# The long and the short pass of each weight block: issued in turn instead of grouped

## What is computed

```python
def swiglu(x, w_in, w_out):
    a, b = jnp.split(x @ w_in, 2, axis=-1)
    return (jax.nn.silu(a) * b) @ w_out

for l in range(DEPTH_2):                                   # 2 layers
    x = x + 0.5 * rmsnorm_2(swiglu(rmsnorm_2(x, ffn1_pre_g[l]), w_ffn1_in[l], w_ffn1_out[l]), ffn1_post_g[l])
    h = rmsnorm_2(x, mix_pre_g[l])
    (z, xbc, dt_raw, rq, rk, rv, rg, aq, ak, av, gate) = jnp.split(h @ w_in[l], offsets, axis=-1)
    ...                                                    # three mixers: y_ssd, y_ret, y_att
    ys = jnp.stack([y_ssd.astype(x.dtype), y_ret.astype(x.dtype), y_att.astype(x.dtype)], axis=2)
    branch = jnp.einsum('blmc,mcd->blmd', ys, w_branch[l])
    gates = jax.nn.sigmoid((gate + b_gate[l]).reshape(bsz, L, N_BRANCH, D_MODEL))
    y = jnp.sum(gates * branch, axis=2) @ w_out[l]
    x = x + rmsnorm_2(y, mix_post_g[l])
    x = x + 0.5 * rmsnorm_2(swiglu(rmsnorm_2(x, ffn2_pre_g[l]), w_ffn2_in[l], w_ffn2_out[l]), ffn2_post_g[l])
```

## Time and profile before

| | |
|---|---|
| time, median of 3 runs | 2068.77 us (2067.3 to 2069.11) |
| span of the profiled execution | 2065.9 us |
| PE busy | 1909.0 us, 92% |
| PEld busy | 1529.2 us, 74% |
| DVE busy | 1163.1 us, 56% |
| ACT busy | 897.5 us, 43% |
| DMA, mean | 235 GB/s |
| the chain that ended last, by engine | PE 77%, DMA 18% |

### The profile page before, as it was taken

How to read it: one execution, slowest core, us unless ns; L and a number is a source line. 1 busy time by engine, 2 the same in 40 slices (tenths; PEclk the granted TensorE clock), 3 DMA queues, 4 the chain that set the end, 5 groups by cost and what they waited for, 6 DMA issues and landing times.

```text
span 2065.9 us, 29171 instructions
## 1 busy us (share of the span) xinstructions
PE 1909.0 (92%) x11974; PEld 1529.2 (74%) x11974; DVE 1163.1 (56%) x1632; ACT 897.5 (43%) x1338; POOL 43.8 (2%) x99
## 2 busy tenths in 40 slices
PE   8998666766689999999999999999999999999998
PEld 8983222212168888999988988888888999889887
DVE  5761111100056756568876776476674779766763
ACT  5531000000044544568653654454444677645542
POOL 0010000000010000000000000000000000000000
PEclk9999888888799999999999999999999999999999
DMA  8489999999983655534444555445555434455552
GB/s 329 181 329 388 425 428 426 426 427 426 427 352 128 256 187 184 185 122 144 153 171 176 206 187 199 163 165 215 193 183 183 164 123 154 147 180 207 185 194 90
DMA packets 58001, 486.00 MB, mean 235 GB/s; under 512 B 6464, under 2 KB 6464, under 8 KB 7712
## 3 DMA queue, kind: packets, MB, share of 16 engines
q1 hardware_dynamic: 56736, 476.24, 60.6%
q0 software_dynamic: 1152, 8.16, 1.0%
HBM read 483.33 MB, written 1.05 MB: 234 GB/s over the span
## 4 chain that ended last, share of the span: by engine, by line
PE 77%; DMA 18%; ACT 1%; DVE 1%; issue 1%; SPq 0%; POOL 0%; DVEq 0%; ACTq 0%; POOLq 0%
DMA ring<-in_w_experts 16%; PE bank L1644 16%; PE bank L1659 12%; PE bank L1764 11%; PE bank L2022 8%; PE bank L1657 7%; PE bank L1678 4%; PE bank L1694 3%; PE bank L1676 2%; DMA work<-in_w_experts 2%; PE bank L1655 2%; PE bank L1479 1%; PE bank L1127 1%; ACT work L2508 1%; PE bank L1674 1%; PE bank L2229 1%
## 5 line engine op out<-in xcount | busy, mean ns | idle before, releaser
L1617 DVE TENSOR_TENSOR ring_parts<-ring,work_parts 128x2048 fp32r<-128x2048 f32 x168 | 384.5, 2291 | 184.5 <-ACT work_parts L1610 155.1
L1610 ACT ACTIVATE work_parts<-ring 128x2048 fp32r<-128x2048 f32 x118 | 224.9, 1911 | 105.5 <-PE bank L1764 76.7
L1659 PE MATMUL bank<-work_parts 128*128 128x512 f32 x840 | 213.2, 393 | 0.0
L1644 PE MATMUL bank<-pair_parts,ring_parts 128*128 128x256 f32 x672 | 189.9, 283 | 0.0
L1657 PEld LDWEIGHTS bank<-work_parts,ring_parts 128*128 128x128 f32 x1280 | 174.6, 190 | 12.3
L1657 PE MATMUL bank<-work_parts,ring_parts 128*128 128x256 f32 x1280 | 178.5, 282 | 0.0
L1659 PEld LDWEIGHTS bank<-work_parts 128*128 128x128 f32 x840 | 150.1, 189 | 26.2
L1764 PE MATMUL bank<-work_parts 128*128 128x512 f32 x512 | 161.5, 389 | 0.0
L1617 DVE TENSOR_TENSOR ring_parts<-ring,columns_parts 128x2048 fp32r<-128x2048 f32 x56 | 128.3, 2290 | 53.0 <-ACT columns_parts L1610 25.1
L1405 DVE TENSOR_TENSOR work<-work,bank 128x512 f32<-128x512 f32 x8 | 5.5, 688 | 251.8 <-PE bank L1479 251.8
L1479 PE MATMUL bank<-work 128*32 128x512 f32 x512 | 85.5, 804 | 61.6 <-DMA work<-in_w_experts 61.6
(11 more groups left out here) (451 smaller groups left out, 3713.3 us busy)
## 6 DMA issues: line engine op xcount, KB each, us to landing
ring<-in_w_layers SPq DMA_DIRECT2D x242, 1024.0 KB, 4.9
work<-in_w_experts SPq DMA_DIRECT2D x42, 2048.0 KB, 36.2
ring<-in_w_experts SPq DMA_DIRECT2D x36, 1024.0 KB, 23.2
ring<-in_w_experts SPq DMA_DIRECT2D x14, 2048.0 KB, 37.4
work<-in_w_experts SPq DMA_DIRECT2D x20, 1024.0 KB, 10.1
ring<-in_w_first SPq DMA_DIRECT2D x16, 1024.0 KB, 7.9
tail<-in_w_experts SPq DMA_DIRECT2D x7, 2048.0 KB, 40.5
columns<-in_w_experts SPq DMA_DIRECT2D x8, 1024.0 KB, 42.0
```

Of the source, the lines that this page charges most:

```text
L1610: act.activation(his[j % len(his)], m.ring[U.slot(names[j])], ACT.Copy).then_inc(F["unit_hi"], 1)
L1617: dve.tensor_tensor(m.ring_r[slot], m.ring[slot], his[j % len(his)].bitcast(F32), ALU.subtract).then_inc(F["unit_lo"], 1)
L1644: mm = pe.matmul(out, w, x, start=k + n == 0, stop=k == KT - 1 and n == 2)
L1659: mm = pe.matmul(bank[:], hi[:, k, :], both[:, k, :], start=False, stop=k == KT - 1)
```

## The change

In both functions the loop over the weight blocks issues the long and the short matmul of the same block one after the other. The first long one still starts the sum; the last instruction of a job, which ends the sum and carries the semaphore, is now the short one of `k` = 7. The number of matmuls and of weight loads, their operands, the bank, the claim of the bank and the wait for the parts stay.

```diff
@@ wide_columns
-        pe.matmul(bank[:], hi[:, 0, :], both[:, 0, :], start=True, stop=False)
         for k in range(KT):
-            pe.matmul(bank[:, 0:T], lo[:, k, :], both[:, k, 0:T], start=False, stop=False)
-        for k in range(1, KT):
-            mm = pe.matmul(bank[:], hi[:, k, :], both[:, k, :], start=False, stop=k == KT - 1)
+            pe.matmul(bank[:], hi[:, k, :], both[:, k, :], start=k == 0, stop=False)
+            mm = pe.matmul(bank[:, 0:T], lo[:, k, :], both[:, k, 0:T], start=False, stop=k == KT - 1)
         mm.then_inc(B.full(job), 1)
@@ wide_end
-        pe.matmul(halves, hi[:, 0, :], both[0], start=True, stop=False)
         for k in range(KT):
-            pe.matmul(halves[:, first], lo[:, k, :], both[k][:, first], start=False, stop=False)
-        for k in range(1, KT):
-            mm = pe.matmul(halves, hi[:, k, :], both[k], start=False, stop=k == KT - 1)
+            pe.matmul(halves, hi[:, k, :], both[k], start=k == 0, stop=False)
+            mm = pe.matmul(halves[:, first], lo[:, k, :], both[k][:, first], start=False, stop=k == KT - 1)
         mm.then_inc(B.full(job), 1)
```

## The result

| | before | changed |
|---|---|---|
| time, median of 12 runs | 2068.54 us (2065.36 to 2071.16) | 2072.04 us (2066.05 to 2076.74) |
| span of the profiled execution | 2065.9 us | 2068.7 us |
| ratio | | 1.0019, 95% interval 1.0010 to 1.0027 |

The change makes the kernel slower by 0.19%, 3.5 us between the medians. The forecast was 2064.4 us, the range 2053 to 2071.

The account below looks back on a forecast made before the run. The prediction took PE's rate of taking matmuls as the bound: 1696 pairs falling from 349.2 to 346.6 ns save 4.4 us, so 2068.77 - 4.4 = 2064.4 us, range 2053 to 2071.

Parts of the forecast that it names:

- The bound: In the FFN input, gates and branches stretches, the rate at which PE takes matmuls alone sets the end.
- the count of 1696 pairs: In `wide_columns` and `wide_end`, 212 jobs of 8 pairs, each one long and one short matmul, make 1696 pairs.
- the cover: In the first FFN, low parts are ready under 2 us ahead; PE arriving 0.54 us earlier still fits.
- The price of a pair: A long and a short in turn fall from 349.2 to 346.6 ns, saving 4.4 us over all pairs; chance 0.45.
- two readings: For 346.6 ns: settled rates 226.7 + 119.9, or border prices, short 6 ns under and long 7 over, cancelling.
- The third row: At L1181 and L1182, two and two in turn take 655 ns a round, the sum of their separate rates.
- Rival (c): Each long behind a short keeps 233.7 ns, shorts 119.8: 353.5 a pair, 7.3 us more, 2076.1 us; chance 0.15.
- prices that cancel: At changes of kind, the short's gain offsets the long's loss; mean durations near 276 to 278 and 396 ns.
- Rival (a): Loads hide fully, every short costs 113.7 ns and long 226.7: 340.4 a pair, 14.9 us less; chance 0.22.
- The rule of the Trainium skill: Loads hide behind shorts as behind longs, so both orders cost the same: no change, 2068.8 us.
- the two sums: Whole-kernel times with one pair price throughout: 2064.4 us at 346.6 ns, 2076.1 us at 353.5 ns.

Follow-up runs that it names:

- e5: Changed kernel with many job orders in one execution, including two longs, two shorts in turn: jobs wholly in turn 2.773 to 2.774 or 2.812 to 2.832 us.
- e10: Kernel of e6 with the first job of each stretch in the old order (long, 8 shorts, 7 longs) and full weights: 2.733 us per job in all six stretches.
- e6: Changed kernel with long matmuls of blocks 1 to 7 loading 64 instead of 128 weight columns: 2.733 us per job in FFNs, 2.773 in gates and branches.
- e8: Changed kernel, each stretch's first job long, 8 shorts, 7 longs, second with two doubled runs: 2063.89 us, ratio 0.9977 to the kernel before.
- e9: Changed kernel with the first job of each stretch in the old order (long, 8 shorts, 7 longs): 2073.4 us, ratio 1.0026 to the kernel before.

## Why the prediction was wrong, step by step

- **The bound, the count of 1696 pairs, the cover.** Right. PE has no wait in the stretches, neither for low parts nor for a transfer, at either rate.
- **The price of a pair, 346.6 ns.** This is the step that failed, in the sentence that two readings meet there. The sum is right for the quick rhythm to a tenth of a ns (2.773 us a job was what the prediction asked the trace to show), partly by luck, since its terms are not: 231.8 + 114.8 on average instead of 226.7 + 119.9. And it was taken for the price of the stream. I added up rates that belong to runs of one kind and to first places behind such runs, and took it for granted that a stream without runs would settle at their sum. It does not settle at one price: it has at least two rates that keep themselves, and five stretches of six took the other, 353.3. The kernel before gave a sign of this: behind the eight shorts the seven longs that start at 1157.61 us take 233, 236, 228, 233, 231, 226 and 227 ns. The cost of a long there depends on more than the matmul just ahead of it, and two prices for two neighbours leave that out.
- **The third row, L1181 and L1182.** It shows whole 4-byte operands in twos, with rates that sum. It was read as a rule on kinds in turn. Two and two of the split operands (e5) comes to 2.787 us a job, 348.3 ns a pair, above the sum; the row did not carry over.
- **Rival (c), 353.5.** Its price is the measured one within 0.2 ns, but not its mechanism: no long stays at 233.7 with a short at 119.8. The rhythm goes through three pairs of 350, 361 and 349 ns. The mean durations that were to tell the cases apart don't name it: 281 and 399 ns in the slow stretch at 1343 to 1453 us (283 and 396 were foretold for (c)), 277 and 394 in the quick one at 1154 to 1262 us (276 to 278 and 396 were foretold for prices that cancel). Against its full 7.3 us stands the one stretch that ran quick; 4.9 us of both together is seen in the trace. I gave it 0.15 because the two prices don't stand side by side before; that was an argument about the neighbours of a matmul, and neighbours alone don't decide.
- **Rival (a), 340.4.** No stretch came to it with full loads, so a short that has no run of shorts ahead of it is not at 113.7 for that reason alone. With half the load beneath the short the pair does come to 340 ns, in all six stretches of e10 and in the FFNs of e6. The gates and branches of e6, at 346.7 with the same loads, show that the load alone does not decide either.
- **The rule of the Trainium skill** in "TensorE: Matmul & The Clock Gate", section "LDWEIGHTS (loading the stationary operand)", puts a load at columns / 1.2 ns, an estimate of 107 ns for 128 columns. The prediction drew from it that a load hides and that the order makes no difference. The runs disagree: the order alone moves a job between 2.773 and 2.827 us (e8, e9), and half a load beneath the short takes it to 2.733 (e10).
- **The range.** It left out (c) and ended at 2071; the time is 2072.04. It lies between the two sums, 2064.4 and 2076.1, because one stretch ran at one rate and five at the other; no forecast with one price for all stretches gives it.

## What to carry to other kernels

Where two kinds of matmul alternate, don't trust a cost of the pair that is summed from runs of each kind: in this kernel the stream locks into one of several rhythms, and the few matmuls ahead of it decide which. When the same code runs at different rates in different stretches of one trace, with no wait and one clock, vary the few instructions ahead of the stretch before blaming buffers or traffic; many entries can be tried in one execution, and the best one kept. The old order, with its 7 longs in each job, costs 20 ns a job more than the quick rhythm, but costs the same in every stretch.

## What the runs showed of the hardware that was not expected

- Matmuls with 128 columns of weights, 512 and 256 columns in turn, run at 346.7 or at 353.3 ns a pair at one granted clock (1.00), each kept to the end of its stretch (73 us in the gates and branches, 111 to 113 us in the FFN inputs). The slow pattern repeats in 1.06 us, three pairs, and is 20 ns longer than three quick pairs; the old order loses the same 20 ns once per job of eight pairs (2.793 against 2.773).
- With 64 instead of 128 columns of weights loaded beneath the short pass, pairs come to 340 ns, which is 226.7 + 113.3 (e10 throughout, e6 in the FFNs alone).
- The same code behind the same matmuls can enter either rhythm. In all four FFN stretches of both profiles of the changed kernel the eight matmuls ahead stand at the same distances to 1 ns; the first long then takes 313 ns in the stretch that runs quick and 314 to 318 ns in the three that run slow.
- **Open:** what PE carries from one matmul to the next is in no record. The load starts about 3 ns after the matmul ahead of it in either rhythm. Why the second FFN of layer 0 enters quick by itself in both profiles of the changed kernel was not tried; the 1 to 5 ns in its first long are seen, not explained. Nor is it known whether all timed runs of the changed kernel had one quick stretch; their times spread wider (2066 to 2077 us) than those of the kernel before (2065 to 2071).
